# Seventh weight operand of chunk 0 in a slot of its own, and the last tiles' block sums behind GpSimd's splits

## The reference, cut to what matters

```
def sq_relu_ffn(h, w1, w2):
    return jnp.square(jax.nn.relu(h @ w1)) @ w2      # w1 1024 x 4096, w2 4096 x 1024
...
xp = xp + sq_relu_ffn(rms_norm(xp, norm_ffn_g[i]), w_ffn1[i], w_ffn2[i])
xs = xs + sq_relu_ffn(rms_norm(xs, norm_ffn_g[i]), w_ffn1[i], w_ffn2[i])
```

## Time and profile before

| what | value |
|---|---|
| runs | 2540.52, 2544.1, 2545.16 us; median 2544.1 |
| the profiled execution: its own time | 2545.7 us |
| its span in the profile | 2544.0 us |
| mean granted TensorE clock | 0.986 of full |
| busy share PE, DVE, ACT, POOL | 97%, 58%, 31%, 56% |

### The profile page before, as it was taken

The page is one execution under the profiler, slowest core; times in us unless marked ns, Lnnn a source line. Parts: engine busy times, 40 slices in busy tenths (PEclk is TensorE's granted clock), DMA queues, the critical chain, the costliest instruction groups (busy, mean ns, idle before and its releaser), DMA issues.

```text
span 2544.0 us, 42346 instructions
## 1 busy us (share of the span) xinstructions
PE 2455.3 (97%) x17227; PEld 2321.4 (91%) x17227; DVE 1464.3 (58%) x1980; ACT 777.2 (31%) x1164; POOL 1413.5 (56%) x1043
## 2 busy tenths in 40 slices
PE   8999999999999998999989999989999999989998
PEld 7998866999999998999978998669999999989998
DVE  4324389444334356777868878764433433667777
ACT  4200168321101033333238832652100000333331
POOL 4433256255445468787952343953454543888784
PEclk9999999999999999999999998999999999999999
DMA  6111120212443344444140111002144334534531
GB/s 218 40 50 35 42 95 2 85 50 102 151 151 131 121 191 158 159 127 159 56 147 18 51 34 55 18 18 102 34 152 151 126 126 168 196 125 145 159 127 77
DMA packets 128201, 264.10 MB, mean 104 GB/s; under 512 B 15517, under 2 KB 81141, under 8 KB 123478
## 3 DMA queue, kind: packets, MB, share of 16 engines
q1 hardware_dynamic: 125446, 245.17, 28.2%
q10 hardware_dynamic: 2640, 17.31, 1.7%
HBM read 173.72 MB, written 87.93 MB: 103 GB/s over the span
## 4 chain that ended last, share of the span: by engine, by line
PE 66%; POOL 15%; issue 9%; DVE 6%; ACT 2%; DMA 1%; SPq 0%; POOLq 0%; DVEq 0%; ACTq 0%
PE PS L278 51%; POOL w L2151 8%; PE PS L322 4%; PE PS L1099 1%; PE PS L1160 1%; POOL stage L2143 1%; POOL stage L2141 1%; PE PS L1510 1%; PE PS L1137 1%; POOL stage L2145 1%; PE PS L1539 1%; PE PS L1479 1%; POOL stage L2147 1%; POOL Lb L1874 1%; DMA hid_spill<-ob 1%
## 5 line engine op out<-in xcount | busy, mean ns | idle before, releaser
L278 PE MATMUL PS<-h,w_sp 128*128 128x352 f32 (+1 forms) x5184 | 861.3, 326 | 18.4 <-DVE h L728 6.6
L278 PEld LDWEIGHTS PS<-h,w_sp 128*128 128x128 f32 (+1 forms) x5184 | 842.7, 189 | 26.2 <-issue 20.2
L2109 POOL TENSOR_TENSOR w_sp<-stage,ones 128x512 fp32r<-128x512 f32 x244 | 265.6, 1120 | 838.9 <-PE PS L278 791.6
L322 PE MATMUL PS<-Bq,w 128*128 128x264 f32 x5376 | 663.5, 286 | 24.3 <-DVE xT L475 23.1
L322 PEld LDWEIGHTS PS<-Bq,w 128*128 128x128 f32 x5376 | 661.0, 190 | 26.7 <-DVE xT L475 19.4
L278 PE MATMUL PS<-hz,w_sp 128*128 128x352 f32 x3456 | 567.0, 323 | 0.0
L278 PEld LDWEIGHTS PS<-hz,w_sp 128*128 128x128 f32 x3456 | 557.7, 188 | 0.0
L2151 POOL TENSOR_TENSOR w<-stage,w 128x512 fp32r<-128x512 f32 x224 | 352.1, 1594 | 142.3 <-ACT w L372 142.3
L2117 POOL TENSOR_TENSOR w_sp<-stage,w_sp 128x512 fp32r<-128x512 f32 x244 | 370.0, 1547 | 0.0
L438 DVE SCALAR_TENSOR_TENSOR ob<-PS,rstd 128x1056 f32<-128x1056 f32 x64 | 80.5, 1257 | 398.0 <-PE PS L278 397.9
L362 ACT ACTIVATE ob<-ob 128x1056 f32<-128x1056 f32 x64 | 69.6, 1087 | 609.9 <-DVE ob L438 609.9
(11 more groups left out here) (309 smaller groups left out, 2210.7 us busy)
## 6 DMA issues: line engine op xcount, KB each, us to landing
hid_spill<-ob SPq DMA_DIRECT2D x32, 2112.0 KB, 7.6
stage<-in_w_ffn SPq DMA_DIRECT2D x64, 1024.0 KB, 7.5
Bq<-hid_spill SPq DMA_DIRECT2D x112, 528.0 KB, 3.7
stage<-in_w_in_even SPq DMA_DIRECT2D x10, 1024.0 KB, 4.9
stage<-in_w_in_odd SPq DMA_DIRECT2D x9, 1024.0 KB, 4.9
x_spill<-xT ACTq DMA_DIRECT2D x2, 4224.0 KB, 12.7
xT<-x_spill ACTq DMA_DIRECT2D x2, 4224.0 KB, 12.5
xtok<-in_x_prompt SPq DMA_DIRECT2D x8, 512.0 KB, 8.9
```

Source lines behind the costliest of these rows:

```text
L278: mm = pe.matmul(out[0:m, c, :], lhs, rhs(k, b)[:, c * CH:(c + 1) * CH], start=(i == 0 and n == 0), stop=(i == nk - 1 and n == 2))
L322: mm = pe.matmul(out[:, c, :], w2[q][i][:, a, m * P:(m + 1) * P], Bq[q][:, b, i, c * QN:(c + 1) * QN], start=(i == 0 and n == 0), stop=(i ...
L2109: pool.tensor_tensor(w_sp[:, s, 0, q:q + 512], stage[:, s, q:q + 512], ones[:, 0:1].to_broadcast([P, 512]), ALU.mult).then_inc(w_hi_done, 1)
```

## The change

The weight operand of product 6 gets, in chunk 0 alone, a place of its own (`w2_first`) in slot 1 of `w_sp`. Its high parts are made after `square(15,1)` and before the five `b_high` of chunk 0; the wait ahead of them is now that for the last up job, and the wait for the store of `ob[1]` moves to the first use of `w2[6]`, in chunk 1. POOL makes the split of product 6 before `last_combine`.

```
+        w2_first = [at(f"w2_first_{i}", o_w + 4 * UN * 4 + 4096 * i, [P, 2, 512], F32R) for i in range(2)]
+
+        def w2_of(c, q, i):
+
+            return w2_first[i] if c == 0 and q == 6 else w2[q][i]
...
     (down_tile, w_high and split_down take w2_of(c, q, i) in place of w2[q][i])
...
                     if q == 0 and not first:
                         b_high(c - 1, 6, d)
+                    if q == 6 and first:
+                        act.wait_ge(hid_st[1], 16 * (8 * L + 8))
                     w_high(c, q, d)
...
             square(15, 1)
+            act.wait_ge(job_done, j0 + 32)
+            w_high(0, 6)
             for q in range(2, 7):
                 b_high(0, q)
-            act.wait_ge(hid_st[1], 16 * (8 * L + 8))
-            w_high(0, 6)
             prepare(1, first=True)
...
             def down_all(L):
-                split_down(0, L, qs=range(6))
+                split_down(0, L)
                 last_combine(L)
-                split_down(0, L, qs=(6,))
                 with pool.Fori(0, 7) as i:
                     split_down(1, L, i)
```

More of the change, by code:

```diff
@@ L313, in pair_banks, with down_tile @@
             return PS[:, b:b + 2, 0:QN]
-        def down_tile(pe, L, t, q, m, dt=0):
+        def down_tile(pe, L, t, q, m, dt=0, c0=1):
             pe.wait_ge(pt_free, PT_L * L + t - 3 + dt) if PT_L * L + t >= 4 else None
@@ L321, in down_tile @@
                     for c in range(2):
-                        mm = pe.matmul(out[:, c, :], w2[q][i][:, a, m * P:(m + 1) * P],
+                        mm = pe.matmul(out[:, c, :], w2_of(c0, q, i)[:, a, m * P:(m + 1) * P],
                                        Bq[q][:, b, i, c * QN:(c + 1) * QN], start=(i == 0 and n == 0),
@@ L339, in chunk @@
                             evacuated(pe, j0 + 31)
-                        down_tile(pe, L, 28 * c + 4 * q + m, q, m, d * 28)
+                        down_tile(pe, L, 28 * c + 4 * q + m, q, m, d * 28, c)
             chunk(0)
@@ L371, in w_high @@
                         act.wait_ge(v_stage[i], 16 * (K + 1) + d * 16)
-                    act.activation(w2[q][i][:, 0, :], stage[:, i, 512 * A_AT[q]:512 * A_AT[q] + 512],
+                    act.activation(w2_of(c, q, i)[:, 0, :], stage[:, i, 512 * A_AT[q]:512 * A_AT[q] + 512],
                                    ACT.Copy).then_inc(wh_done, 1)
@@ L2150, in split_down @@
                         pool.wait_ge(wh_done, 14 * K + 2 * q + i + 1 + d * 14)
-                        pool.tensor_tensor(w2[q][i][:, 1, :], stage[:, i, 512 * A_AT[q]:512 * A_AT[q] + 512],
-                                           w2[q][i][:, 0, :].bitcast(F32), ALU.subtract).then_inc(wl_done, 1)
+                        pool.tensor_tensor(w2_of(c, q, i)[:, 1, :], stage[:, i, 512 * A_AT[q]:512 * A_AT[q] + 512],
+                                           w2_of(c, q, i)[:, 0, :].bitcast(F32), ALU.subtract).then_inc(wl_done, 1)
             def last_combine(L):
```

## The result

The changed kernel takes **2547.46 us** (median of 20 runs, 2545.81 to 2548.79) against 2543.92 us of the kernel before (20 runs, 2540.52 to 2547.72). The ratio is 1.0013, with a 95% interval of 1.0007 to 1.0019: 3.5 us slower, within 0.2% of no change but outside the noise. The profiled execution took 2546.65 us, its span is 2544.9.

What follows compares the result with a forecast made beforehand. The bound was taken as the moment chunk 1 starts plus the clock lost there. Second landings +0.4 and +1.5 us and clock +0.8 gave +2.7, so 2546.8 us on the median 2544.1; range 2538.5 to 2552.0.

Steps and rivals of the forecast that it cites:

- The store's start: Issue of store(15) behind GpSimd's block sums: at least 945.4 in layer 0, 945.9 taken; 2201.5 taken in layer 1.
- From the store to the second landing: SP queue: chunk 1's second weight load lands 12.5 to 14.4 us behind the store's issue, 13.5 taken.
- the store does not hold the loads: Rival on SP's queue: loads run beside the store and need their old time, -7.6 to -10 us; chance 0.11.
- From the landing to chunk 1: GpSimd work between the second weight load's landing and chunk 1's start: 21.6 us, untouched by the change.
- the stall: TensorE's wait ahead of product 2 of chunk 0: 1 or 5 us, costed at nothing as covered by slack.
- The clock: TensorE's half clock behind a longer gap ahead of chunk 1: +0.8 us, bounds -6.0 to +1.6.
- the seams: Stretches from each down product's first matmul to chunk 1's start; second landings, hence chunk 1, +1.9 us together.
- Ahead of product 2: Chunk 0: VectorE's low part comes late, TensorE waits 1 us or 5; taken at nothing, with 11.9 us slack.
- A later store: Rival: VectorE's turns delay GpSimd's sums and the store, each us reaching chunk 1's start in full; 2551.6 us, chance 0.13.

Runs made afterwards that it cites:

- e1: Changed kernel with the own slot kept, but GpSimd's block sums before the product 6 split and ScalarE's five hidden high parts first, as before; 2535.0 us.
- e4: Changed kernel with SP's two weight loads of chunk 1 issued ahead of store(15); 2535.59 us, ratio 0.9968 to the kernel before.
- e3: Changed kernel with two more subtractions on GpSimd, into spare bytes, between the third and fourth block sum; 2552.14 us.
- e6: Changed kernel with one more wait on GpSimd, for its own last low part, ahead of the four block sums; 2544.91 us.
- e5: Changed kernel with chunk 1's two weight loads ahead of store(15) and ScalarE's high parts of hidden operands 2 and 3 ahead of w_high(0,6); 2534.68 us.
- e7: Changed kernel with chunk 1's two weight loads and the hidden operands of its products 0 and 1 ahead of store(15); 2535.33 us.
- e2: Changed kernel with ScalarE's high parts of hidden operands 2 and 3 moved ahead of w_high(0,6); 2546.89 us.
- e8: Changed kernel with the edits of e6 and e7 together; 2525.38 us, ratio 0.9924 to the kernel before.
- e9: As e8, but with the hidden operands of products 0 and 1 of chunk 1 behind store(15) again; 2532.73 us.
- e10: The kernel of e8 once more, beside e9 on the same chip; 2525.38 us.

## Why the prediction was right, point by point

- **The sign, the size and the place** held: 2546.8 us were forecast, 2547.46 measured. I gave 0.70 to "within 0.2%", and the ratio is 1.0013.
- **The store's start**, 945.9 taken: 945.43, the low bound; in layer 1 2201.45. VectorE was not let in a second time (the first three sums took 1.3 us each), so the row of 4.40 us was a better guide here than the rule of the Trainium skill ("SBUF — State Buffer", section "Who interferes with whom").
- **From the store to the second landing**, 13.5 taken: 13.4 and 13.9 us (958.79 - 945.43, 2215.37 - 2201.45); 13.2 and 14.2 in e1. This was the deciding step, and e4 shows that it was: with the loads ahead of the store the time fell by 11.9 us, and the gap ahead of chunk 1 went from 5.80 to 0.89 us in layer 0. The rival "the store does not hold the loads" is out, and not by a small distance: behind the store the loads took 10.4 and 12.5 us from issue to landing in layer 0 of the changed kernel, ahead of it 4.7 and 6.1 in e4.
- **From the landing to chunk 1**, 21.6 us, "none of it touched by the change": this step failed. It was 23.45 us in layer 0 and 22.9 in layer 1. The low parts for products 5 and 6 of chunk 0 (the row at 959.05 above) were made ahead of the second landing before the change and behind it now. With those for products 0 and 1 of chunk 1 (964.95) and product 2 (973.70), VectorE now took five turns in GpSimd's work instead of three (in layer 1 the first of the five fell mostly ahead of that work). Before, DVE and then POOL:

```profile
952.46 2.42 DVE L465 TENSOR_TENSOR Bq<-Bq 128x1056 fp32r<-128x1056 f32 x2
959.73 8.28 POOL L2151 TENSOR_TENSOR w<-stage,w 128x512 fp32r<-128x512 f32 x5 [2.37 <-ACT w L372]
967.97 2.51 POOL L2141 TENSOR_TENSOR stage<-stage 128x512 f32<-128x512 f32 x2
```

POOL in the changed kernel:

```profile
959.50 9.01 POOL L2159 TENSOR_TENSOR w<-stage,w 128x512 fp32r<-128x512 f32 x5 [1.16 <-ACT w L378]
968.47 3.55 POOL L2149 TENSOR_TENSOR stage<-stage 128x512 f32<-128x512 f32 x2
```

In e3 and e6, where the low parts for products 5 and 6 were done when that work began, as they had been before the change, it was 21.7. So I had costed the stall at nothing because its 5 us were covered; its other effect, on when VectorE's next work meets GpSimd, was not.
- **The clock**, +0.8 us taken: it had the wrong sign, -0.3 and -1.1 us. The gap ahead of chunk 1 became shorter (5.80 and 5.83 us), not longer, as the stall took part of it. Half clock appeared behind the stall instead, under cover: 192 matmuls in 25.04 us. So the total is partly luck: over both layers the chain from the landing was 3.1 us longer than reckoned, and the clock 2.2 us better (-1.4 for +0.8). Reckoned from the first matmul of each down product, the second landings came 1.0 us sooner than forecast over both layers, so that the seams grew by 3.9 us for the 1.9 forecast.
- **Ahead of product 2** I had named 1 us or 5; it was 5. That it would be paid in full if the cover went is what e4, e5 and e7 show, and half clock on top.
- **A later store** costs time as the rival said, but not "in full". Reckoned from the first matmul, the store of e3 goes out 3.6 and 3.7 us later than in the changed kernel and the second load lands 3.0 and 3.7 us later, but the seams grow by 1.3 and 2.4 only, as the work behind the landing is 1.7 and 1.2 us shorter; the time is 4.7 us longer.

## What to carry to other kernels

A wait that is removed pays only as far as the next thing in each in-order list allows: here SP's list put a 2112 KB store ahead of the loads that had been freed, and the work moved aside had delayed that very store. Write down, for the transfer that ends the wait, what stands ahead of it on its queue and when that can go, and try the order of the queue before that of the engines. And when a stall is called covered, look also at what it delays on the engines behind it, and price it again, with its clock, for the kernel in which the cover is gone.

## What the runs showed of the hardware

VectorE instructions with two inputs in SBUF were kept out by a GpSimd that works without a pause, for far longer than one instruction: 4.40 us before, 5.78 after, 9.32 in e2, over three, four and seven GpSimd instructions, where 1.24 is the time without company. The Trainium skill ("SBUF — State Buffer", section "Who interferes with whom") lets the later one wait until the first has finished; the trace agrees with that in the turns of chunk 1, where a low part takes 1.9 to 2.4 us, and with layer 1 of e4, but not in these rows. Without a pause ahead of the sums the long form came in 11 of 12 layers profiled (the changed kernel, e2, e3, e4, e5 and e7), and with GpSimd's old order in all four (the kernel before and e1, 4.4 us); with GpSimd's wait for its own last result it came in none of 8 (e6, e8, e9, e10). What decides between the two forms is open: the runs show only that the pause settles it.
